# A chunked delta-rule recurrence: the level masks move to GpSimd, the level copies are shared by VectorE and ScalarE, and two groups of products change place on TensorE

## The reference, cut to what matters

```python
def step(S, inp):                       # per head, S is 64 x 64
    r_t, w_t, k_t, v_t, kk_t, kka_t = inp
    sa = jnp.einsum('bhvk,bhk->bhv', S, kk_t)
    S = (S * w_t[:, :, None, :] - sa[..., None] * kka_t[:, :, None, :]
         + v_t[..., None] * k_t[:, :, None, :])
    y_t = jnp.einsum('bhvk,bhk->bhv', S, r_t)
...
y = wkv7_scan(rh, heads(decay), kh, vh, kk, kk * ah)
y = head_group_norm(y, lnx_w.astype(f32), lnx_b.astype(f32))
bonus = (jnp.sum(rh * kh * r_k.astype(f32), axis=-1, keepdims=True) * vh)
y = (y + bonus.reshape(bsz, t, D_INNER)) * jax.nn.silu(g.astype(f32))
```

## Time and profile before

| | |
|---|---|
| median of 3 runs | 2051.74 us (2047.96 to 2052.86) |
| the profiled execution: time | 2047.91 us |
| its span in the trace | 2045.9 us |
| TensorE, VectorE, ScalarE, GpSimd busy | 92%, 61%, 43%, 14% of the span |
| first and last L1364 (one for each step) | 276.2 and 815.4 us |
| one step, 563.11 to 598.89 us | 35.78 us |

### The profile page before, as it was taken

How to read it: one execution, slowest core, us unless ns; L and a number is a source line. 1 busy time by engine, 2 the same in 40 slices (tenths; PEclk the granted TensorE clock), 3 DMA queues, 4 the chain that set the end, 5 groups by cost and what they waited for, 6 DMA issues and landing times.

```text
span 2045.9 us, 43870 instructions
## 1 busy us (share of the span) xinstructions
PE 1886.3 (92%) x18912; PEld 1475.6 (72%) x18912; DVE 1253.5 (61%) x1787; ACT 884.2 (43%) x1368; POOL 294.1 (14%) x282
## 2 busy tenths in 40 slices
PE   4999779999999999899999999999888699999997
PEld 3677657676777767578888888887665478888885
DVE  6572168787777777544555554546557677787522
ACT  5342255646656466433222222334445354444321
POOL 3000033543535444400000000000000000000000
PEclk9999889999999999999999999999999799999998
DMA  3224311111111111143322223322110032223331
GB/s 123 78 83 139 104 42 45 42 45 41 46 30 42 45 42 39 43 151 97 103 94 94 102 93 101 96 93 73 52 42 21 21 114 98 97 93 103 91 93 64
DMA packets 51454, 154.15 MB, mean 75 GB/s; under 512 B 8512, under 2 KB 11072, under 8 KB 51264
## 3 DMA queue, kind: packets, MB, share of 16 engines
q1 hardware_dynamic: 51264, 151.35, 22.8%
HBM read 145.04 MB, written 6.29 MB: 74 GB/s over the span
## 4 chain that ended last, share of the span: by engine, by line
PE 51%; DVE 4%; ACT 1%; issue 0%; DMA 0%; DVEq 0%; ACTq 0%
PE bank L1653 15%; PE bank L1654 15%; PE bank L1652 15%; PE bank L1740 1%; PE bank L1741 1%; PE bank L1742 1%; DVE room L2364 0%; PE bank L1777 0%; DVE room L2331 0%; PE bank L1760 0%; PE bank L1821 0%; PE bank L1812 0%; PE bank L1723 0%; PE bank L1788 0%; PE bank L1785 0%
## 5 line engine op out<-in xcount | busy, mean ns | idle before, releaser
L1859 ACT ACTIVATE w_hi<-raw 128x1024 fp32r<-128x1024 f32 (+2 forms) x195 | 197.8, 1015 | 499.5 <-PE bank L1654 457.0
L1652 PE MATMUL bank<-h_hi,w_hi 128*128 128x512 f32 x896 | 349.8, 390 | 0.0
L1654 PE MATMUL bank<-h_hi,w_lo 128*128 128x512 f32 x896 | 348.6, 389 | 0.0
L1653 PE MATMUL bank<-h_lo,w_hi 128*128 128x512 f32 x896 | 348.6, 389 | 0.0
L151 DVE TENSOR_TENSOR w_lo<-raw,w_hi 128x1024 fp32r<-128x1024 f32 (+2 forms) x202 | 236.2, 1170 | 155.2 <-ACT w_hi L1859 154.7
L1652 PEld LDWEIGHTS bank<-h_hi,w_hi 128*128 128x128 f32 x896 | 168.2, 188 | 35.7 <-issue 0.7
L1653 PEld LDWEIGHTS bank<-h_lo,w_hi 128*128 128x128 f32 x896 | 168.2, 188 | 35.5 <-issue 0.7
L1654 PEld LDWEIGHTS bank<-h_hi,w_lo 128*128 128x128 f32 x896 | 168.2, 188 | 34.9
L144 PE MATMUL bank<-xg_hi,g_hi 128*128 128x512 f32 x256 | 104.4, 408 | 21.6 <-DVE g_lo L151 11.8
L814 ACT ACTIVATE swapT<-invT 64x256 f32<-64x256 f32 x192 | 79.8, 415 | 83.3 <-DVE invT L1367 41.1
L1634 POOL TENSOR_SCALAR room<-room 128x512 f32<-128x512 f32 x4 | 3.5, 884 | 696.7 <-ACT room L1928 696.7
(11 more groups left out here) (389 smaller groups left out, 4301.3 us busy)
## 6 DMA issues: line engine op xcount, KB each, us to landing
raw<-in_w_conv SPq DMA_DIRECT2D x64, 512.0 KB, 3.2
raw<-in_w_up SPq DMA_DIRECT2D x44, 512.0 KB, 3.2
raw<-in_w_out SPq DMA_DIRECT2D x32, 512.0 KB, 3.8
raw<-in_w_in SPq DMA_DIRECT2D x20, 512.0 KB, 3.2
g_raw<-in_w_g SPq DMA_DIRECT2D x16, 512.0 KB, 3.2
g_raw<-in_w_r SPq DMA_DIRECT2D x16, 512.0 KB, 3.8
w_k<-in_w_k SPq DMA_DIRECT2D x16, 512.0 KB, 4.1
w_v<-in_w_v SPq DMA_DIRECT2D x16, 512.0 KB, 3.6
```

The source lines that it names most:

```text
L1652: pe.matmul(to, whi, hi, start=begin, stop=False)
L1653: pe.matmul(to, whi, lo, start=False, stop=False)
L1654: last = pe.matmul(to, wlo, hi, start=False, stop=end)
L1859: act.activation(w_hi[:, g % RING, 0:width], raw[:, g % RAW, 0:width], ACT.Copy).then_inc(S("whi"), 1)
```

## The change

The masks for the levels were put to the product A V, which lies in PSUM. They are now put to A itself, in SBUF, by GpSimd: `level(c, lv)` multiplies the A half of LA by the (transposed) mask of level `lv` into one of two LEVEL tiles, in turn. The two lie in the memory of NTG. `low_products` reads LEVEL in place of LA. What then lies in PSUM needs no mask, only a copy: for levels 0 to 3 VectorE copies head 0's half (`masked_low`) and ScalarE head 1's (`head_low`); level 4 is copied whole by VectorE.

The bonus was one operation of VectorE (L1301, sum times value). Now ScalarE copies the sum out of PSUM (`bonus_copy`) and GpSimd multiplies (`bonuses`, at the step's start). `rate` is cut off `prepare` and comes behind the split of ysq on GpSimd. The second mask of MK goes behind the first level's copy on VectorE. ScalarE evacuates the mixed values ahead of a table load rather than behind it. On TensorE `mixed_values` moves ahead of the last `low_products`, and the own outputs move ahead of the last `up_products`; two pieces of the value projection move from behind the NTG product to ahead of it.

```diff
-    put("level_mask", np.concatenate([twice(below(1 << k)) for k in range(1, LVL)], 1))
+    put("level_mask", np.concatenate([twice(below(1 << k).T) for k in range(1, LVL)], 1))
...
+        LEVEL = [nc.alloc_sbuf_tensor_at(f"level{n}", [P, 2, TB, HD], F32, offset=ntg_at + 4 * T * n) for n in range(2)]
+        SHARED = 4
...
+            def rate(n):
                 pool.wait_ge(S("kfac"), n + 1)
                 apart(pool)
                 pool.tensor_scalar(tha[:, :], tha[:, :], 0.5, 0.5, ALU.mult, ALU.add).then_inc(S("a"), 1)
...
+            def bonuses(n, p):
+                pool.wait_ge(S("bsum"), n + 1)
+                pool.wait_ge(S("vT"), n + 1)
+                apart(pool)
+                pool.tensor_tensor(bonus[:, p, :], bonus[:, p, :], vT[:, :], ALU.mult).then_inc(S("bonus"), 1)
+
+            def level(c, lv):
+                pool.wait_ge(S("la"), 2 * c + 2)
+                if lv > 1:
+                    pool.wait_ge(S("low_mm"), LV * c + lv - 1)
+                apart(pool)
+                pool.tensor_tensor(LEVEL[lv % 2][:, :, :, :], LA[:, :, :, 0, :],
+                                   over2(C["level_mask"][:, lv * HD:(lv + 1) * HD]), ALU.mult).then_inc(S("level"), 1)
...
+                level(c, 0)
+                level(c, 1)
+                bonuses(c, q)
+                level(c, 2)
+                if last:
+                    out_halves(range(8))
+                level(c, 3)
+                level(c, 4)
                 if not last:
                     key_halves(c + 1)
                     prepare(c + 1, 1 - q)
                 if last:
-                    pool.wait_ge(S("inv0"), 2 * IC)
-                    out_halves(range(10))
+                    out_halves(range(8, 10))
                 if c > 0:
                     halved("ysq", c - 1)
+                if not last:
+                    rate(c + 1)
...
+            def bonus_copy(n, p):
+                act.wait_ge(S("bsum_mm"), n + 1)
+                need(act, S("plus"), n - 1)
+                act.activation(bonus[:, p, :], GK[:, :], ACT.Copy).then_inc(S("bsum"), 1)
...
+            def head_low(c, lv):
+                act.wait_ge(S("low_mm"), LV * c + lv + 1)
+                act.activation(low[:, 1, :, :], thin(X[1][:, 0:half]), ACT.Copy).then_inc(S("low1"), 1)
...
                 swapped(c, 3)
+                head_low(c, 3)
                 turned(c, 2)
...
                 swapped(c, 4)
-                act.preload_act_table_set("natural_log")
                 act.wait_ge(S("mv_mm"), c + 1)
                 for h, from_ in enumerate((ROT[1], GV)):
                     act.activation(XK[:, :, h, HD:P], thin(from_[:, 0:half]), ACT.Copy).then_inc(S("mv"), 1)
+                act.preload_act_table_set("natural_log")
...
                 pe.wait_ge(S("inv"), inv_count(c, lv))
+                pe.wait_ge(S("level"), LV * c + lv + 1)
...
-                            m = pe.matmul(X[h][rows[j ^ h], cols(b)], LA[rows[j], h, b, 0, :], inv[rows[j], h, b, :],
+                            m = pe.matmul(X[h][rows[j ^ h], cols(b)], LEVEL[lv % 2][rows[j], h, b, :], inv[rows[j], h, b, :],
...
                 pe.wait_ge(S("low"), LV * c + lv + 1)
+                if lv < SHARED:
+                    pe.wait_ge(S("low1"), SHARED * c + lv + 1)
...
                     key_sums(c + 1)
                 else:
                     fill(keys, 0, 3)
+                mixed_values(c)

                 low_products(c, 4)
-                mixed_values(c)
-                up_products(c, 4)
-                fill(keys, 0, 3)
-                if not first:
-                    variances(c - 1)
-
                 need(pe, S("ysq"), c)
...
-                fill(values, 2, 3)
+                up_products(c, 4)
+                fill(keys, 0, 3)
+                if not first:
+                    variances(c - 1)
+                fill(values, 4, 3)
...
-                fill(values, 12, 9)
+                fill(values, 10, 9)
...
-                    dve.tensor_tensor(low[:, :, :, :], heads(0), over2(C["level_mask"][:, lv * HD:(lv + 1) * HD]),
-                                      ALU.mult).then_inc(S("low"), 1)
+                    if lv < SHARED:
+                        dve.tensor_copy(low[:, 0, :, :], thin(X[0][:, 0:half])).then_inc(S("low"), 1)
+                    else:
+                        dve.tensor_copy(low[:, :, :, :], heads(0)).then_inc(S("low"), 1)
...
-                for h in range(2):
-                    masked(MK[:, h], ROT[h][:, :], "mk")
+                masked(MK[:, 0], ROT[0][:, :], "mk")

                 masked_low(0)
                 states(2)
+                masked(MK[:, 1], ROT[1][:, :], "mk")
```

More of the change, by code:

```diff
@@ L557, in rwkv_phase @@
         XK = sbt(ctx, "XK", [P, TB, 2, P])
+        ntg_at = -(-nc.sbuf_base // 32) * 32
         NTG = sbt(ctx, "NTG", [P, TB, 2, P])
+        LEVEL = [nc.alloc_sbuf_tensor_at(f"level{n}", [P, 2, TB, HD], F32, offset=ntg_at + 4 * T * n) for n in range(2)]
+        SHARED = 4
         tok = {n: sbt(ctx, f"{n}_tok", [P, TB, P]) for n in ("kd", "be", "v")}
@@ L726, in _ @@
             prepare(0, 0)
+            rate(0)
             read_halves(0)
@@ L839, in step @@
                 swapped(c, 0)
+                head_low(c, 0)
                 if last:
-                    y_whole(8, 9, 10, 11, 12, 13)
+                    y_whole(8, 9, 10)
+                swapped(c, 1)
+                head_low(c, 1)
+                if last:
+                    y_whole(11, 12, 13)
                 turned(c, 0)
-                swapped(c, 1)
                 swapped(c, 2)
+                head_low(c, 2)
                 turned(c, 1)
@@ L885, in step @@
                 if not last:
+                    bonus_copy(c + 1, 1 - q)
                     values(c + 1)
@@ L906, in _ @@
             split(1, "k")
+            bonus_copy(0, 0)
             values(0)
@@ L924, in dense @@
                             pe.wait_ge(S("wlo_k"), n + 1)
-                            need(pe, S("bonus"), n)
+                            need(pe, S("bsum"), n)
                         else:
@@ L1058, in projected @@
                         if n == 0:
-                            pe.wait_ge(S("bonus"), IC)
+                            pe.wait_ge(S("bsum"), IC)
                         else:
@@ L1295, in removals @@
                 dve.tensor_tensor(bet[:, :], tha[:, :], cum[:, :], ALU.mult).then_inc(S("bet"), 1)
-            def bonuses(n, p):
-                dve.wait_ge(S("bsum_mm"), n + 1)
-                dve.wait_ge(S("vT"), n + 1)
-                need(dve, S("plus"), n - 1)
-                dve.tensor_tensor(bonus[:, p, :], GK[:, :], vT[:, :], ALU.mult).then_inc(S("bonus"), 1)
             def finished(c, p):
@@ L1435, in step @@
                         out_split(0)
-                    bonuses(c + 1, 1 - q)
             split(0, "k", 0, 1)
@@ L1451, in _ @@
             split(1, "k", 0, 1)
-            bonuses(0, 0)
             run(step)(dve)
```

## The result

The changed kernel takes 2076.26 us (median of 4 runs, 2070.91 to 2078.41) against 2049.85 us before (4 runs). The ratio is 1.0113, with an interval from 1.0092 to 1.0135: slower. The forecast was 2074.

What follows compares the result with a forecast made beforehand. TensorE, busy for 92% of the span, was taken as the bound. First level 11.5, ScalarE 8.8 and last step 3 sum to 23.3 us, giving 2071.2 or 2075.0, taken as 2074; range 2064 to 2086, chance 0.50.

Steps and rivals of the forecast that it cites:

- The first level: GpSimd's mask blocks VectorE's second invT operation, 0.69 to 1.66 us; less the bonus, 0.72 us a step, 11.5 us in all.
- The bonus: Ahead of LA's masks on VectorE: moving it off masks LA 0.25 us sooner (0 to 0.6).
- ScalarE: Level 3's half copy delays be_tok 0.99 us; NTG's product starts 0.63 us later (0.02 to 1.0), 8.8 us over 14 steps.
- the prediction's list: Places where TensorE would wait for ScalarE: L1177, for swapT, and L1189, for NTG.
- The products: At levels 3 and 4, moved products close waits of 1.62 us, which turn into waits for ScalarE: gain 0.
- the three waits: TensorE's waits: 0.21 us before level 3's second product, 0.98 for inv and 0.43 for low at level 4; together 1.62 us.
- rival C: GpSimd becomes the bound: masks at 2.6 us, or its later finish blocks kap and bet; 2090 to 2112 us, chance 0.16.
- The last step: Eight out_halves on GpSimd ahead of level 3's mask make its product 2 us later; y_lo's pieces wait too: +3 (0 to 6).
- A: No blocking at the first level: VectorE's L1364 and L1367 run at 0.69 us; +8 us, 2059, chance 0.18.
- B: Faster: ScalarE has unseen slack between be_tok and NTG, the 1.62 us stay closed; 2027 or 2041 us, chance 0.16.

Runs made afterwards that it cites:

- both probes: Kernel before plus one unused GpSimd operation a step on LA's half: two SBUF inputs (mask) 2066.31 us, ratio 1.0073; one input (copy) 2055.38 us, ratio 1.0002.
- the run with both cures: Changed kernel with level 0 masked by VectorE, GpSimd's masks begun behind the first transpose, and level 3 copied whole by VectorE: 2053.71 us, ratio 1.0001 to before.
- The cure tried for it: Changed kernel, in the last step only two of GpSimd's eight low halves ahead of level 3's mask, six behind it: 2074.40 us, ratio 1.0117 to before.
- the changed kernel with the old products: Changed kernel with TensorE's order of the last level and ScalarE's table load put back as before: 2073.29 us, ratio 1.0096 to before.
- level 0 by VectorE: Changed kernel, level 0 masked out of PSUM by VectorE, GpSimd's masks of levels 1 to 4 behind the first transpose: 2063.24 us, ratio 1.0055 to before.

## Why the prediction was right

**The first level: right in place and size.** The step was "at the first level `inv` is 0.97 - 0.25 = 0.72 us later", all of it on the path. L1367's successor takes 1.67 us (1.66 forecast); the wait is 0.94 us (0.9 forecast). The blocking by itself is 0.97 us in the shortest step when it is taken away, 1.0 when it is put into the kernel before. The bonus gave 0.16 rather than 0.25. Net 0.81 a step (0.72 forecast). In the Trainium skill, GPSIMD Engine Reference, Key points, VectorE instructions with two SBUF inputs are said to contend with GpSimd; both probes agree, 0.69 us became 1.67 and 0.98.

**ScalarE: right in mechanism, wrong in where it shows.** `be_tok` starts 0.95 us later than it did (0.99 forecast), and ScalarE's chain is late by 0.74 at NTG's end. But L1236, which reads NTG, doesn't wait; TensorE stands for ScalarE earlier, before `key_sums` (0.95 us) and before L1224 (0.81). `key_sums` was not in the prediction's list. Taking the copy off ScalarE gave 0.75 us a step, against 0.63.

**The products: the step that failed.** "These 1.62 us turn into waits for ScalarE; a gain of 0." Two errors in it. The own outputs take the place of `mixed_values` as what fills the wait for `low`, so that wait stays, 0.44 us: the three waits never were 1.62 us to be had. And the move does win, 0.52 us in an undisturbed step of the changed kernel, 0.23 in the kernel before. The parts of the change, each from an experiment's shortest step, make 0.97 (level 0) + 0.75 (ScalarE) - 0.16 (bonus) - 0.23 (products) = 1.33 us a step, and 1.27 is measured. The total came out near the forecast's 0.72 + 0.63 = 1.35 by luck: the first level costs 0.09 and ScalarE 0.12 more, and the products give 0.23 where nothing was expected. The sum hangs on which gain of the products is put in: with 0.52 it would be 1.04. For 0.23 speaks the run with both cures: its step is 0.43 us under the kernel before, and bonus and products make 0.39.

**The steps beyond the undisturbed ones.** Before, GpSimd's finishing work blocks `kap` and `bet` in four steps (rival C's mechanism): three take 36.6 us, the last 38.05. A fourth step of 36.6 us holds the stop of 1.3 us at L930. In the four, `gate` starts 0.3 us ahead of `bet`, in the others 3.0 us behind it. After the change it is 2.8 to 3.3 us behind in every step, and none is blocked. The kernel before spends 539.2 - 15 x 35.27 = 10 us beyond undisturbed steps, the changed one 557.5 - 15 x 36.54 = 9 us. One nuisance went, the holes came, and the sum stayed; the forecast had neither.

**The last step: right in sign, wrong in its first reason.** +3 forecast, +4.3 measured. The forecast worked out 2 us of it from a late mask of level 3 and announced a wait for GpSimd there. TensorE shows none; the 3.2 us that it waits more are for the low halves, which the forecast named second. The cure tried for it failed.

**The rivals.** A (no blocking) is out by 1.67 us in 16 of 16 steps. B (ScalarE has slack) is out by the run with level 3 on VectorE. C (GpSimd is the bound) is out: a repeated mask and 64-element pieces cost nothing extra, 1287 ns in the median, where I had kept 2.6 us as an end; and `kap` and `bet` were never blocked.

**Sum.** 23.3 us was forecast. 18.3 for the steps, 4.3 for the last and -1.6 for the start make 21.0 in the trace; the medians differ by 26.4, and the untouched part's scatter is of the size of the rest.

What stays open: why TensorE's instruction packets start late at some places; why the holes are few in the kernel before and in the one with the bonus moved, 2.3 us, but more with each other edit, the probes' 4.5 and 5.1 among them. With one trace a kernel, it isn't shown that this follows the kernel and not the execution. Nor is it shown how much of the timed difference is theirs, since they can be seen in profiled executions only.

## What to carry to other kernels

Work given to an idle engine is not free when its operands sit in SBUF: look at what the neighbour does in the same microsecond, and price it by a pair of rows in the trace that already shows the two together. An engine with a low busy share can be without slack in one stretch; find the chain between its last wait and the next product that reads from it, and count the spare time there (0.36 us here) before adding 0.38. Split a change of many parts: here two parts gain and two lose more. And where an engine stops without a wait, count its instructions up to there: a fixed distance between such stops tells more than their times.

## What the runs showed of the hardware that was not expected

- A running one-input GpSimd copy of 0.76 us also holds up a two-input VectorE operation, by 0.29 us.
- The blocking goes the other way too. In ten steps of the kernel before, GpSimd's one-input operation on `yc` takes 2.2 us in place of 0.77, and VectorE's two-input operations in a row beside it take their 0.69 each. So GpSimd let VectorE pass there and got in between L1407 and L1410, which are 0.04 us apart:

```profile
521.43 2.20 POOL L696 TENSOR_SCALAR yc<-yc,mixpar 128x512 f32<-128x512 f32 x1 [0.18 <-POOL yc L693]
521.87 0.69 DVE L1288 TENSOR_TENSOR kap<-kk,decays 128x512 f32<-128x512 f32 x1
522.47 0.69 DVE L1295 TENSOR_TENSOR bet<-tha,cum 128x512 f32<-128x512 f32 x1
```

- GpSimd multiplies 128x512 by a mask that repeats over 64 columns, from strided 64-element pieces, in 1287 ns, as long as a plain product.
- TensorE stands for up to 2.5 us inside rows of small products with no wait, always at a multiple of 256 of its records from the last such place, and goes on 1.1 to 1.6 us after a 16 KB instruction packet has ended. Over 15 steps that is 0.9 us in the kernel before, 4.5 and 5.1 with the probes, 6.2 in the changed kernel with the old products, 12.4 in the changed kernel, 15.6 in it with level 0 by VectorE. The sum doesn't follow the timed ratio: the last of these is the faster of the two changed ones.
- A stretch of identical code behind the loop takes 1176.6 to 1185.2 us in the fourteen traces, with the mean granted clock at 0.98 or 0.97. In the 91 timed runs of the kernel before beside the experiments, 2042.8 to 2063.4 us, time and mean granted clock (0.980 to 0.970) go together, with a correlation of -0.86.
